# Gate row by DMA, both heads' scores on two array halves, high part of the probabilities first, table copies moved

## The reference

```
shift, scale, gate = split(silu(c) @ w_ada + b_ada, 3)          # (1024, 3072)
h    = rmsnorm(x, g_norm) * (1 + scale) + shift
proj = h @ w_in                                                 # (1024, 4096)
q, k, v, z_attn, b_g, c_g, h_c, z_conv = split(proj, 8)
q, k = rope(q), rope(k)                                         # 8 heads of 64
y_attn = moba_attention(q, k, v)     # 2 blocks of 256, top 3: plain causal attention here
y_attn = rmsnorm(y_attn, g_attn_out) * silu(z_attn)
y_conv = b_g * conv_w3(c_g * h_c)                               # depthwise, causal
y_conv = rmsnorm(y_conv, g_conv_out) * silu(z_conv)
x = x + gate * (concat(y_attn, y_conv) @ w_out)
out = rmsnorm(x, g_final)
```

## Time and profile before

| | |
|---|---|
| median of 3 runs | 285.13 us (285.10 to 285.28) |
| profiled execution | 284.59 us, span 282.8 us |
| TensorE busy | 268.6 us, 95% |
| TensorE weight loads | 222.1 us, 79% |
| DVE busy | 197.0 us, 70% |
| ACT busy | 141.1 us, 50% |
| POOL busy | 115.0 us, 41% |
| granted TensorE clock | 0.996 of full |
| chain that ended last | TensorE 74% of the span |
| DMA | 43.8 MB, mean 155 GB/s |

### The profile page before, as it was taken

The page is one execution under the profiler, slowest core; times in us unless marked ns, Lnnn a source line. Parts: engine busy times, 40 slices in busy tenths (PEclk is TensorE's granted clock), DMA queues, the critical chain, the costliest instruction groups (busy, mean ns, idle before and its releaser), DMA issues.

```text
span 282.8 us, 3727 instructions
## 1 busy us (share of the span) xinstructions
PE 268.6 (95%) x1292; PEld 222.1 (79%) x1292; DVE 197.0 (70%) x351; ACT 141.1 (50%) x237; POOL 115.0 (41%) x73
## 2 busy tenths in 40 slices
PE   5889999899999999999999999999999999999990
PEld 1567888688888888888888888888888878888880
DVE  4898888799989976889899865922773531305564
ACT  4845355367059733673633364637196583402331
POOL 2500001466433433191363322343356999922410
PEclk9999999999999999999999999999999999999998
DMA  5999944296702462067334102332503444500113
GB/s 204 381 417 419 406 186 129 72 418 203 255 3 74 122 194 96 0 233 288 112 82 141 52 27 74 111 72 96 206 14 137 153 145 167 206 0 2 75 74 149
DMA packets 12405, 43.82 MB, mean 155 GB/s; under 512 B 2145, under 2 KB 2145, under 8 KB 10978
## 3 DMA queue, kind: packets, MB, share of 16 engines
q1 hardware_dynamic: 12242, 43.32, 43.0%
q10 hardware_dynamic: 144, 0.26, 0.2%
HBM read 38.33 MB, written 2.10 MB: 143 GB/s over the span
## 4 chain that ended last, share of the span: by engine, by line
PE 74%; ACT 6%; issue 6%; POOL 4%; DVE 4%; DMA 3%; SPq 1%; POOLq 0%; ACTq 0%; DVEq 0%
PE ps L1009 17%; PE ps L1011 17%; PE ps L1010 17%; PE ps L1068 4%; POOL w_lo L579 3%; PE ps L1153 3%; PE ps L1083 2%; PE ps L1145 2%; DMA xt<-in_x 2%; PE ps L1089 2%; DVE mod_junk L688 2%; PE ps L1081 1%; PE ps L1087 1%; PE ps L1128 1%; PE ps L1127 1%
## 5 line engine op out<-in xcount | busy, mean ns | idle before, releaser
L579 POOL TENSOR_TENSOR w_lo<-raw,w_hi 128x1024 fp32r<-128x1024 f32 x29 | 74.1, 2559 | 123.8 <-ACT w_hi L327 123.7
L1009 PE MATMUL ps<-h_lo,w_hi 128*128 128x512 f32 x200 | 78.9, 395 | 0.0
L1011 PE MATMUL ps<-h_hi,w_hi 128*128 128x512 f32 x200 | 78.0, 390 | 0.0
L1010 PE MATMUL ps<-h_hi,w_lo 128*128 128x512 f32 x200 | 77.9, 389 | 0.0
L1011 PEld LDWEIGHTS ps<-h_hi,w_hi 128*128 128x128 f32 x200 | 37.6, 188 | 8.0
L1010 PEld LDWEIGHTS ps<-h_hi,w_lo 128*128 128x128 f32 x200 | 37.6, 188 | 7.2
L1009 PEld LDWEIGHTS ps<-h_lo,w_hi 128*128 128x128 f32 x200 | 37.6, 188 | 7.1
L688 DVE CUSTOM_DVE_ANT_0 mod_junk<-ada,c_bc 128x1024 f32<-128x1024 f32 x22 | 34.1, 1549 | 1.1
L327 ACT ACTIVATE w_hi<-raw 128x1024 fp32r<-128x1024 f32 x29 | 30.4, 1051 | 6.9 <-DMA raw<-in_wslots 6.9
L394 ACT ACTIVATE probs<-probs,rmin 128x384 f32<-128x384 f32 (+3 forms) x32 | 17.6, 552 | 30.0 <-DVE rmin L814 30.0
L824 DVE TENSOR_SCALAR probs<-probs,prec 128x384 f32<-128x384 f32 (+3 forms) x32 | 21.4, 733 | 0.3
(11 more groups left out here) (153 smaller groups left out, 503.3 us busy)
## 6 DMA issues: line engine op xcount, KB each, us to landing
raw<-in_wslots SPq DMA_DIRECT2D x33, 512.0 KB, 3.4
ada<-in_ada SPq DMA_DIRECT2D x11, 1024.0 KB, 8.9
raw<-in_whead SPq DMA_DIRECT2D x8, 448.0 KB, 7.2
xt<-in_x SPq DMA_DIRECT2D x4, 512.0 KB, 4.9
x<-in_x SPq DMA_DIRECT2D x4, 512.0 KB, 5.8
out<-x SPq DMA_DIRECT2D x3, 512.0 KB, 2.7
ada<-in_ada SPq DMA_DIRECT2D x2, 512.0 KB, 8.0
qs<-q_lo SPq DMA_DIRECT2D x16, 64.0 KB, 2.0
```

The source lines that it names most:

```text
L579: nc.gpsimd.tensor_tensor(lo, src[:, :], hi.bitcast(F32), ALU.subtract).then_inc(s_lo, 1)
L1009: nc.tensor.matmul(o, a_hi, b_lo, start=start, stop=False)
L1010: nc.tensor.matmul(o, a_lo, b_hi, start=False, stop=False)
L1011: return nc.tensor.matmul(o, a_hi, b_hi, start=False, stop=stop)
```

## The change

- **Gate row by DMA.** `gate_rows`, the `gdiag` products and the two ACT copies leave. The gate columns of `w_ada` and `b_ada` are ordered so that `gcol` is [128, 8] with channel 8p + k. SP writes it to a DRAM tensor behind slot 20's load and reads it back, broadcast to 128 partitions, before `gfin`.
- **Scores.** ACT and DVE write q's and k's two parts once (`qt`, `kt`). Four DMAs each (`heads_together`) regroup 32-row blocks so that partitions 0 to 63 hold head 0 of the pair and 64 to 127 head 1. `score(p)` forms three terms (lo x hi, hi x lo, hi x hi) with 64 rows, the heads alternating, head 0 into banks 2 to 4, head 1 into banks 5 to 7. It stands where `score(p, 0)` stood, and `least(p, 1)` follows `least(p, 0)` directly. `transpose_probs(p, 0)` waits for both heads' minima.
- **High part first.** `values` runs four matmuls on `pt_hi`, which wait for `p_hi` alone, then waits for `p_lo` and runs four on `pt_lo`.
- **Table copies.** On ACT the last scaling of `xt` goes before `sin_t`, and `cos_t` goes behind the first `h_hi`. Head operands run in the order 0, 5, 6, 3, 4, 1, 2.
- **POOL** waits for the last modulation half of the head (`mod_step` 16) before slot 0.
- **Tail.** The sum of two partial squares into `ss2[12]` moves ahead of the last residual.

```diff
+            def heads_together(dst, src, done):
+                for of, to in ((0, 0), (32, 64), (64, 32), (96, 96)):
+                    sp.dma_start(dst[to:to + 32, :, :].bitcast(F32), src[of:of + 32, :, :].bitcast(F32)).then_inc(done, 16)
+            def regroup_q(p):
+                sp.wait_ge(q_split, p + 1)
+                sp.wait_ge(qk_lo, 2 * p + 1)
+                sp.wait_ge(scores, 6 * p)
+                heads_together(qd, qt, dup_q)
...
+                if n == 20:
+                    sp.wait_ge(gcol_ok, 1)
+                    sp.dma_start(gate_d, gcol[:, :]).then_inc(gate_out, 16)
                 if n == NU - 1:
+                    sp.wait_ge(gate_out, 16)
+                    sp.dma_start(gate[:, :], gate_d.rearrange("p k -> (p k)").partition_broadcast(P)).then_inc(gate_in, 16)
...
             square_x(3)
+            act.wait_ge(x_rstd, TT)
+            nc.scalar.activation(xt[:, TT - 1, :], xt[:, TT - 1, :], ACT.Copy, scale=rstd[:, TT - 1:TT]).then_inc(x_norm3, 1)
             act.wait_ge(trig_tr, 1)
             nc.scalar.activation(sin_t[:, :], bank(2), ACT.Copy, scale=prm[:, C_SIGN:C_SIGN + 1]).then_inc(trig_ok, 1)
-            nc.scalar.activation(cos_t[:, :], bank(3), ACT.Copy).then_inc(trig_ok, 1)
-            act.wait_ge(x_rstd, TT)
-            nc.scalar.activation(xt[:, TT - 1, :], xt[:, TT - 1, :], ACT.Copy, scale=rstd[:, TT - 1:TT]).then_inc(x_norm3, 1)
...
+                if j == 0:
+                    nc.scalar.activation(cos_t[:, :], bank(3), ACT.Copy).then_inc(trig_ok, 1)
...
-            for i in range(2):
-                act.wait_ge(gate_bc, i + 1)
-                nc.scalar.activation(gate[:, i * BANK:(i + 1) * BANK], bank(5 + i), ACT.Copy).then_inc(gate_ok, 1)
...
+            pool.wait_ge(mod_step, 2 * KT)
             for n in range(12):
                 slot(n)
...
+                operands = list(head_operands(j))
+                for n in (0, 5, 6, 3, 4, 1, 2):
+                    o, a_hi, _, b_hi, _, _ = operands[n]
+                    if j == 0 and n in (3, 4):
+                        pe.wait_ge(cb_ok, n - 2)
+                    if j == 0 and n in (1, 2):
+                        pe.wait_ge(trig_ok, n)
...
+            def score(p):
                 pe.wait_ge(dup_q, 64 * p + 64)
+                pe.wait_ge(dup_k, 64 * p + 64)
+                if p:
                     pe.wait_ge(y_attn, 2 * p)
+                    pe.wait_ge(p_lo, 2 * p)
...
+                    for term, (a, b) in enumerate(((1, 0), (0, 1), (0, 0))):
+                        for h in range(2):
+                            rows = slice(HD * h, HD * h + HD)
+                            o = ps[:, SB[h] + S_AT[i]:SB[h] + S_AT[i] + w]
+                            ins = nc.tensor.matmul(o, qd[rows, a, t], kd[rows, b, 0:w], start=(term == 0), stop=(term == 2))
+                            if n and term == 2:
+                                ins.then_inc(scores, 1)
...
-                pe.wait_ge(p_lo, 2 * p + h + 1)
+                pe.wait_ge(p_hi, 2 * p + h + 1)
                 pe.wait_ge(row_min, 8 * p + 8)
-                for j in range(TT):
-                    for n, pt in enumerate((pt_lo, pt_hi)):
+                for n, pt in enumerate((pt_hi, pt_lo)):
+                    if n:
+                        pe.wait_ge(p_lo, 2 * p + h + 1)
+                    for j in range(TT):
...
+                if e == 8:
+                    dve.wait_ge(x2_sq, 8)
+                    nc.vector.tensor_scalar(ss2[:, 12:13], ss2[:, 6:7], ss2[:, 7:8], None, ALU.add).then_inc(gcol_ok, 1)
                 residual(e)
```

More of the change, by code:

```diff
@@ L253, in _, with regroup_k @@
                     load_ada(j + 1)
[L254 to L270, removed]
+            def heads_together(dst, src, done):
[6 more added lines that the diff above has]
+                heads_together(qd, qt, dup_q)
+            def regroup_k(p):
+                sp.wait_ge(k_split, p + 1)
+                sp.wait_ge(qk_lo, 2 * p + 2)
+                sp.wait_ge(scores, 6 * p)
+                heads_together(kd, kt, dup_k)
             for n in range(NSLOT):
@@ L358, in q_high @@
                 act.wait_ge(rope_r, 2 * p + 1)
-                act.wait_ge(scores, 6 * p)
-                for h in range(2):
-                    nc.scalar.activation(qs[:, h], rq[:, :], ACT.Copy, scale=-(HD ** -0.5)).then_inc(q_split, 1)
+                act.wait_ge(dup_q, 64 * p)
+                nc.scalar.activation(qt[:, 0], rq[:, :], ACT.Copy, scale=-(HD ** -0.5)).then_inc(q_split, 1)
             def k_high(p):
                 act.wait_ge(rope_r, 2 * p + 2)
-                act.wait_ge(scores, 6 * p)
-                for h in range(2):
-                    nc.scalar.activation(kd_hi[:, h], rk[:, :], ACT.Copy).then_inc(k_split, 1)
+                act.wait_ge(dup_k, 64 * p)
+                nc.scalar.activation(kt[:, 0], rk[:, :], ACT.Copy).then_inc(k_split, 1)
             def value_high(m):
@@ L754, in q_low @@
             def q_low(p):
-                dve.wait_ge(q_split, 2 * p + 2)
+                dve.wait_ge(q_split, p + 1)
                 dve.wait_ge(rope_r, 2 * p + 1)
                 dve.wait_ge(dup_q, 64 * p)
-                nc.vector.scalar_tensor_tensor(out=q_lo[:, :], in0=rq[:, :], scalar=-(HD ** -0.5),
-                                               in1=qs[:, 0].bitcast(F32), op0=ALU.mult, op1=ALU.subtract
+                nc.vector.scalar_tensor_tensor(out=qt[:, 1], in0=rq[:, :], scalar=-(HD ** -0.5),
+                                               in1=qt[:, 0].bitcast(F32), op0=ALU.mult, op1=ALU.subtract
                                                ).then_inc(qk_lo, 1)
             def k_low(p):
-                dve.wait_ge(k_split, 2 * p + 2)
+                dve.wait_ge(k_split, p + 1)
                 dve.wait_ge(rope_r, 2 * p + 2)
-                for h in range(2):
-                    nc.vector.tensor_tensor(kd_lo[:, h], rk[:, :], kd_hi[:, h].bitcast(F32), ALU.subtract
-                                            ).then_inc(qk_lo, 1)
+                dve.wait_ge(dup_k, 64 * p)
+                nc.vector.tensor_tensor(kt[:, 1], rk[:, :], kt[:, 0].bitcast(F32), ALU.subtract).then_inc(qk_lo, 1)
             def value_low(m):
@@ L909, in _ @@
                                     prm[:, C_B + 2 * KT:C_B + 3 * KT], ALU.add).then_inc(gcol_ok, 1)
[L910 to L913, removed]
             least(2, 0)
+            least(2, 1)
             conv_taps(2)
             normalise(2, 0)
-            least(2, 1)
             conv_out(2)
@@ L970, in sum_out @@
                 if m == TT - 1:
-                    nc.vector.tensor_scalar(ss2[:, 12:13], ss2[:, e:e + 1], ss2[:, e + 1:e + 2], None, ALU.add
-                                            ).then_inc(gcol_ok, 1)
                     dve.wait_ge(last_sq, 1)
@@ L1156, in values @@
                 ins.then_inc(pv_out, 1)
-            def gate_rows():
-                pe.wait_ge(gdiag_ok, 1)
-                pe.wait_ge(p_lo, 4)
-                for i in range(2):
-                    for j in range(4):
-                        ins = nc.tensor.matmul(bank(5 + i, j * P, (j + 1) * P), ones[:, :], gdiag[:, 4 * i + j, :],
-                                               start=True, stop=True)
-                    ins.then_inc(gate_bc, 1)
             def y_squares(g):
@@ L1201, in _ @@
             unit("Q1")
-            score(0, 0)
+            score(0)
             unit("K1")
-            score(0, 1)
             unit("ZC0")
@@ L1212, in _ @@
             unit("H1")
-            score(1, 0)
+            score(1)
             unit("B1")
-            score(1, 1)
             unit("ZC1")
@@ L1224, in _ @@
             unit("C2")
-            score(2, 0)
+            score(2)
             unit("H2")
-            score(2, 1)
-            gate_rows()
             unit("B2")
@@ L1237, in _ @@
             unit("C3")
-            score(3, 0)
+            score(3)
             unit("H3")
-            score(3, 1)
             unit("B3")
@@ L1304, in host_layout @@
         for two in range(2):
[L1305 to L1306 removed]
+            at = (1 - two) * D + j * P
+            of = slice(at, at + P) if j < 8 else slice(2 * D + 2 * (j - 8) + two, None, 8)
+            ada[j, :, two] = w_ada[:, of].T
     head = np.concatenate([cols("Q0"), cols("K0"), np.arange(start["V"], start["V"] + A), cols("C0")])
```

64 lines of the change are left out of this document (22 added, 42 removed).

## The result

The changed kernel takes 283.40 us (median of 5 runs, 282.86 to 284.16) beside 285.18 for the kernel before on the same chip: a ratio of 0.9941, 95% interval 0.992 to 0.9963. It is 1.8 us faster. The forecast was 280.7 us, 4.4 us less than before; the direction holds, and 2.6 of those 4.4 us are missing. The measured time lies above the forecast's own range (278.5 to 282.0) and inside the wider one that takes in two rivals (up to 284.6). The profiled execution, 284.16 us with a span of 282.1, is the slowest of the five.

A forecast was written before the change was run, and what follows sets the result against it. TensorE's instruction stream was taken to bound the kernel; 1.70 + 1.2 + 0.86 + 0.55 + 0.1 = 4.4 us off 284.59 gave 280.2, a median of 280.7 us, range 278.5 to 282.0, up to 284.6 with two rivals.

The forecast's parts named there:

- two rivals: Score weight loads queuing (0.25, 283.7 us) and POOL getting the port twice before chunk 7 (0.12, 283.0 us).
- the POOL wait: Head chunk 7: holding POOL back unstretches the DVE reduction; 0.55 us of the 1.06 us lost there gained.
- second rival: Head chunk 7: POOL takes the port before both w_lo and h_lo; 2.8 us lost, 283.0 us, chance 0.12.
- own sign of being wrong: Head chunk 7: the forecast is wrong if its second half starts after 56.5.
- The gate row: Gate matmuls leave TensorE's dense stream ahead of pair 2; the DMAs replacing them cost nothing: 1.70 us gained.
- The scores: Score blocks: both row halves run together, with drains at mode changes; 2.26 us a pair, 1.2 us gained.
- Weight loads queue: Score blocks: matmuls overlap but weight loads go one by one; 1.8 us lost, 283.7 us, chance 0.25.
- High part first: Two values calls: high matmuls cover the late pt_lo, ending TensorE waits of 0.33 and 0.53 us; 0.86 gained.
- Table copies and tail: Head: chunk 0 earlier but gain spent before chunk 1, counted 0; tail: sum ahead of last residual, 0.1 us gained.
- gap of 0.6 us or more: Sign before head chunk 1: chunk 0's earlier start would be spent in a wait there.

The follow-up runs named there:

- e3: Changed kernel with POOL's wait for mod_step 16 kept and slot 1 also waiting for DVE's last h_lo of the head: 280.46 us.
- e8: e2 with eight fp32 matmuls of 128 columns, read by nobody, put back on TensorE ahead of pair 2's transposes: 281.78 us.
- e6: e2 with values again waiting for pt_lo and running low and high part in turn for each key tile: 280.89 us.
- e2: Changed kernel with POOL waiting for DVE's last h_lo of the head before slot 0, in place of mod_step 16: 280.13 us.
- e5: e2 with all three score terms of head 0 before those of head 1 inside each query tile: 280.03 us.
- e9: e2 with all twelve score matmuls of head 0 before those of head 1, softmax counts adapted: 286.35 us.

## Why the prediction was right or wrong

**The step that failed is the POOL wait**, the term of 0.55 us gained. The prediction put it as "If `w_lo` goes first, POOL runs 52.3 to 54.7 and `h_lo` ends at 55.3 [...] I take 0.55 gained". What happened is its own second rival: POOL took the port ahead of `w_lo` and again ahead of `h_lo`. In place of 0.55 us gained, the profiled execution has 2.9 lost between chunk 6's last matmul and the first unit (9.08 for 6.15). The prediction's own sign of being wrong shows it: chunk 7's second half was to start by 56.5, and starts at 57.55. The rival's sum was right almost to the tenth (2.8 us lost in the chunk forecast, 2.62 measured). Its chance was wrong, 0.12, and so was the argument against it, that `w_lo` follows tiny operations directly. The release came with the accumulator read, drawn to 51.20; POOL was in at 51.29, while DVE still had `sh` to do (51.31) before `w_lo` (51.43). What the race would be could be asked of the rows of before: POOL is let go by the end of one DVE instruction, DVE has two short ones in hand, and the one row that showed such a boundary had POOL winning. e3 shows further that the first lost boundary matters little alone. It mattered that a second one was coming, because ACT had brought slot 1 forward.

**A price was missing.** Neither the forecast nor the rival had the clock. Behind the 2.6 us wait TensorE ran at its lower level in part of the runs (by their mean granted clock), which cost 1.3 to 1.5 us in the profiled one. The rival's 283.0 without it stands 0.4 below the median.

**The gate row** was right: e8 gives 1.65 for 1.70, and the first residual, which reads the gate, still waits for TensorE alone, 10.69 us as before. In the trace the row was worth 1.8, since the units behind it gained 0.12 too.

**The scores** were right in mechanism and near in size: 0.21 to 0.24 us a pair in the trace for 0.30 forecast. The parts differ: the extra time at both ends of the block is 0.19 a pair and not 0.34, while the block is 2.12 and not 1.92. Its first matmul of a head stands 0.28 from that head's next for 384 columns, where the second stands 0.17. "Weight loads queue" is refuted as it was priced: the block takes 2.12 us and not 2.67, and 24 loads take 1.99 us together, where one path at the 0.11 us of the earlier trace rows would need 2.6.

**High part first** did what was said: both waits are gone. They were worth 1.1 us in the trace with the slower starts behind them. But this is not this edit's alone, as e6 shows (0.38). The prediction's own remark that the single splits move `pt_lo` earlier should have been followed to its end.

**Table copies and tail.** Chunk 0 began at 16.22 (16.15 before) and chunk 1 at 21.82 (21.62 before). The earlier scaling did not even start chunk 0 sooner, since fill-in matmuls stood in TensorE's stream up to its transposes (the last transpose at 14.78, 14.80 before). So the gap of 0.6 us or more that the prediction named as a sign before chunk 1 is not there: the starts around it stand 0.49 us apart. The tail gave 0.05 for 0.1.

With e2's wait the total of the sum is met, though not each term: 1.8 (gate row) + 0.8 (scores) + 1.1 (`values`) + 0.95 (first unit at 58.14 for 59.09) + 0.05 = 4.7, beside 4.76 between the spans of the two profiles and 5.05 between the medians. That the forecast's 4.4 lies so near owes something to luck: the scores gave less than said, and the gate row, the waits and chunk 7 more.

## What to carry to other kernels

Where two engines hold each other up, as POOL and DVE do here, holding one back moves the collision, and what it moves it onto must be listed: follow the held engine's work instruction by instruction from the new release, and ask at each boundary who is first. Release it by the last operation of the critical run that it can hold up, not by the first; here that turned a 3 us loss into a 1 us gain on the same kernel.

A wait put on a dense stream of matmuls can cost more than its length, since the granted clock may drop behind it: here 2.6 us of wait cost some 4 us in the profiled execution that met it.

Two edits that end the same wait have one gain between them, so price each on the kernel that already has the other.

When totals differ by less than the start of a kernel moves from trace to trace, compare a stretch that leaves the start out.

## What the runs showed that was not expected

- **A matmul on one half of the array can start ahead of earlier ones on the other half.** With the heads in turn (e5), matmuls of the second half start 10 ns behind those of the first, ahead of matmuls that stand before them in the program; in e9 this reached past three and no further. The Trainium skill, TensorE: Matmul & The Clock Gate, section Part 3: Packing small matmuls — row/col tiling, The mechanism, says that matmuls start and end in program order, and only weight loads are pulled forward. The starts of e9 speak against this for matmuls of different halves, and the measurement decides.
- **DVE and POOL held each other up for whole instructions.** A 1.08 us split took 3.21 and a 0.69 us one 2.83 when POOL's 2.4 us split had begun 0.14 and 0.53 us before them; POOL's own took 2.82 at the second meeting.
- **The lower clock after 2.6 us without a matmul** came in some runs of one kernel and not in others (two of five, four of six, by the mean granted clock), and cost 1.0 to 1.8 us.
- **The landing of the first blocks of x** differs by up to 1 us between the traces (third square at 8.3 to 9.5 us), more than several of these edits are worth.
